# Neighbourhood attention on one core: the gate projections before the modulation products, instead of the two interleaved head by head

## The reference, cut to what matters

```python
mod = silu_c @ w_ada[layer] + b_ada[layer]                   # 6 * 1024 columns
sh_m, sc_m, gt_m, sh_f, sc_f, gt_f = jnp.split(mod, 6, axis=-1)
h = _rmsnorm(x, g_mix_pre[layer]) * (1.0 + sc_m[:, None]) + sh_m[:, None]
...
(na_k, na_v, ml_k, ml_v, ml_g, na_q, ml_q, ml_o, gate_na, gate_ml) = _split(h @ w_in[layer], IN_SPLITS)
...
o_na = _neighbourhood_attention(na_q, na_k, na_v, na_kc, na_vc, rpb[layer])
o_ml = _mlstm_branch(...)
merged = (jax.nn.sigmoid(gate_na) * (o_na @ w_branch_na[layer])
          + jax.nn.sigmoid(gate_ml) * (o_ml @ w_branch_ml[layer]))
x = x + gt_m[:, None] * _rmsnorm(merged @ w_out[layer], g_mix_post[layer])
```

## Time and profile before

| | us |
|---|---|
| median of 3 runs | 2588.36 |
| lowest, highest | 2583.66, 2589.1 |
| profiled execution, its own time | 2588.36 |
| its span, first to last instruction | 2586.4 |
| TensorE busy | 2296.2 (89%) |
| VectorE busy | 763.5 (30%) |
| ScalarE busy | 627.7 (24%) |
| the 16 iterations of attention, from the span's start | 255.0 to 385.0 |

### The profile page before, as it was taken

The page is one execution under the profiler, slowest core; times in us unless marked ns, Lnnn a source line. Parts: engine busy times, 40 slices in busy tenths (PEclk is TensorE's granted clock), DMA queues, the critical chain, the costliest instruction groups (busy, mean ns, idle before and its releaser), DMA issues.

```text
span 2586.4 us, 31263 instructions
## 1 busy us (share of the span) xinstructions
PE 2296.2 (89%) x13190; PEld 1587.1 (61%) x13190; DVE 763.5 (30%) x1251; ACT 627.7 (24%) x843; POOL 36.8 (1%) x23
## 2 busy tenths in 40 slices
PE   4999997769988988998899869999799699997997
PEld 2468666643333333333333349998799699986997
DVE  1001224241111111121111145443354445442453
ACT  2101432021101101110111134431343334412432
POOL 2100000010000000000000000000000000000000
PEclk7996999969999999999999979999899799998998
DMA  9434352319999999999999957773154345541542
GB/s 277 69 129 144 129 214 83 132 73 428 428 428 427 427 428 428 426 428 428 426 428 427 410 139 158 157 233 107 66 180 171 124 154 155 191 153 66 181 155 89
DMA packets 135924, 626.96 MB, mean 242 GB/s; under 512 B 11244, under 2 KB 19052, under 8 KB 110956
## 3 DMA queue, kind: packets, MB, share of 16 engines
q1 hardware_dynamic: 128384, 621.92, 63.6%
q0 software_dynamic: 1056, 0.20, 0.7%
q10 hardware_dynamic: 6348, 2.81, 0.5%
HBM read 623.69 MB, written 1.05 MB: 242 GB/s over the span
## 4 chain that ended last, share of the span: by engine, by line
PE 68%; DMA 20%; DVE 5%; ACT 3%; issue 2%; ACTq 1%; SPq 0%; DVEq 0%
DMA ring<-in_w_lin 18%; PE bank L1305 14%; PE bank L1051 12%; PE bank L1405 12%; PE bank L1587 10%; PE bank L1602 5%; PE bank L1066 2%; DMA ring<-in_w_ada 1%; ACTq L759 1%; PE bank L1117 1%; DMA ring<-in_w_in 1%; PE bank L1414 1%; PE bank L1293 1%; PE bank L1318 1%; PE bank L1138 1%
## 5 line engine op out<-in xcount | busy, mean ns | idle before, releaser
L1305 PE MATMUL bank<-ring,arenaA 128*64 128x512 f32 x3072 | 694.0, 602 | 37.8 <-DMA ring<-in_w_lin 26.1
L1305 PEld LDWEIGHTS bank<-ring,arenaA 128*64 128x64 f32 x3072 | 211.4, 138 | 461.5 <-issue 392.0
L1051 PE MATMUL bank<-arenaA,ring 128*128 128x256 f32 (+1 forms) x1408 | 339.8, 402 | 14.5 <-ACT arenaA L660 9.2
L1405 PE MATMUL bank<-arena_rounded,ring_rounded 128*128 128x256 f32 x2688 | 334.5, 285 | 9.3 <-ACT arena_rounded L837 7.9
L1405 PEld LDWEIGHTS bank<-arena_rounded,ring_rounded 128*128 128x128 f32 x2688 | 326.2, 191 | 14.2 <-issue 11.0
L1978 DVE TENSOR_TENSOR ring_rounded<-ring,ring_rounded 128x2048 fp32r<-128x2048 f32 (+1 forms) x140 | 293.4, 2133 | 134.1 <-ACT ring_rounded L829 134.0
L1051 PEld LDWEIGHTS bank<-arenaA,ring 128*128 128x128 f32 x1408 | 270.1, 193 | 86.3 <-issue 36.1
L829 ACT ACTIVATE ring_rounded<-ring 128x2048 fp32r<-128x2048 f32 (+1 forms) x140 | 243.0, 1784 | 317.2 <-DMA ring<-in_w_in 93.0
L1587 PE MATMUL bank<-arena_rounded,ring_rounded 128*128 128x256 f32 x2112 | 256.9, 285 | 8.0 <-ACT arena_rounded L954 8.0
L1587 PEld LDWEIGHTS bank<-arena_rounded,ring_rounded 128*128 128x128 f32 x2112 | 256.5, 193 | 8.6 <-issue 8.6
L1926 DVE TENSOR_SCALAR arenaA<-bank 128x512 f32<-128x512 f32 x32 | 22.1, 691 | 508.3 <-PE bank L1305 508.3
(11 more groups left out here) (338 smaller groups left out, 1640.7 us busy)
## 6 DMA issues: line engine op xcount, KB each, us to landing
ring<-in_w_gate SPq DMA_DIRECT2D x64, 2048.0 KB, 23.1
ring<-in_w_lin SPq DMA_DIRECT2D x64, 2048.0 KB, 25.5
ring<-in_w_down SPq DMA_DIRECT2D x64, 2048.0 KB, 21.5
ring<-in_w_in SPq DMA_DIRECT2D x41, 2048.0 KB, 10.8
ring<-in_w_ada SPq DMA_DIRECT2D x12, 2048.0 KB, 15.3
ring<-in_w_ffn_gate SPq DMA_DIRECT2D x10, 2048.0 KB, 7.9
ring<-in_w_ffn_up SPq DMA_DIRECT2D x10, 2048.0 KB, 7.8
ring<-in_w_ffn_down SPq DMA_DIRECT2D x12, 1536.0 KB, 6.4
```

The lines of the kernel that those rows point to most:

```text
L1051: last = pe.matmul(dst, w[:, c, base + m * P:base + (m + 1) * P], rhs(c), start=(c == 0), stop=(c == kc - 1))
L1305: last = pe.matmul(bank[b][k * SLOTS:(k + 1) * SLOTS, :], lhsT(c), slot(j)[:, c % 4, k * 512:(k + 1) * 512], start=False, stop=(c == DC - ...
L1405: last = pe.matmul(b[:, j * T:(j + 1) * T], w[:, c, m * P:(m + 1) * P], h[:, c, :], start=(part == 0 and c == 0 and j == 0), stop=(part == ...
```

## The change

It moves the filler work. Iterations 0 to 7 now each hold one whole gate group (16 matmuls), emptied by ScalarE in the same iteration. Iterations 8 to 15 each hold one whole modulation slab: `ada(i - 4)` and straight behind it `ada_turn(i - 4)`, with ScalarE's `ada_copy(i - 4)` behind the exponential of i, and VectorE's `modulation(i - 4)` ahead of the reciprocal and scaling of i. The slab list and the group list are put in the same order: four gate slabs and then eight modulation slabs. No arithmetic, no size and no operand changes.

```diff
@@ slabs
-        for k, (nm, c0) in enumerate((("gna0", C_GNA), ("gna1", C_GNA + 512), ("gml0", C_GML), ("gml1", C_GML + 512))):
-            slabs += [(nm, w_in[:, :, c0:c0 + 512])]
-            slabs += [(f"ada{i}", w_ada[:, :, 512 * i:512 * i + 512]) for i in (4 + 2 * k, 5 + 2 * k)]
+                  ("gna0", w_in[:, :, C_GNA:C_GNA + 512]), ("gna1", w_in[:, :, C_GNA + 512:C_GML]),
+                  ("gml0", w_in[:, :, C_GML:C_GML + 512]), ("gml1", w_in[:, :, C_GML + 512:C_GML + 1024])]
+        slabs += [(f"ada{i}", w_ada[:, :, 512 * i:512 * i + 512]) for i in range(4, 12)]
@@ groups
-        for k, name in enumerate(GATES):
-            groups += [("act", name), ("dve", f"ada{4 + k}")]
+        groups += [("act", f"gna{m}") for m in range(4)] + [("act", f"gml{m}") for m in range(4)]
+        groups += [("dve", f"ada{i}") for i in range(4, 12)]
@@ ScalarE, iteration i, behind the exponential of i
-                if qt == 0:
-                    ada_copy(4 + h)
-                else:
-                    if i == 1:
+                if i >= 8:
+                    ada_copy(i - 4)
+                if i < 8:
+                    name = filler[i]
+                    if i == 0:
                         act.wait_ge(sum_done, 1)
-                    dst = (gNA if h < 4 else gML)[:, 2 * (h % 4):2 * (h % 4) + 2, :]
-                    empty(GATES[h], dst, ACT.Sigmoid, src=two)
+                    dst = (gNA if i < 4 else gML)[:, 2 * (i % 4):2 * (i % 4) + 2, :]
+                    empty(name, dst, ACT.Sigmoid, src=two)
@@ TensorE
+            fillers = []
+            for nm, i in [(a, i) for a in ("gna", "gml") for i in range(4)]:
+                def f(nm=nm, i=i):
+                    w = slab(f"{nm}{i // 2}")
+                    pair(f"{nm}{i}", w, i % 2, lat)
+                fillers.append(f)
+            for i in range(4, 12):
+                fillers.append(lambda i=i: (ada(i), ada_turn(i)))
...
-                gate_half(i // 2, i % 2)
-                if i % 2 == 0:
-                    ada(4 + i // 2)
-                else:
-                    ada_turn(4 + i // 2)
+                fillers[i]()
@@ VectorE, iteration i
                 if i + 1 < 2 * NA_H:
                     front(i + 1)
+                if i >= 8:
+                    modulation(i - 4)
                 dve.wait_ge(na_exp, i + 1)
                 link(dve.reciprocal(nst[:, 32 + i:33 + i], nst[:, 32 + i:33 + i]))
                 dve.tensor_scalar(Pna[:, i % 2, :], Pna[:, i % 2, :], nst[:, 32 + i:33 + i], None, ALU.mult).then_inc(na_p, 1)
                 if qt:
-                    modulation(4 + h)
```

More of the change, by code:

```diff
@@ L496, in build @@
                   ("ml_q", w_in[:, :, C_MLQ:C_MLO]), ("ml_o", w_in[:, :, C_MLO:C_GNA]),
-                  ("rel0", A["rel"][:, 0:4096]), ("rel1", A["rel"][:, 4096:8192])]
-        for k, (nm, c0) in enumerate((("gna0", C_GNA), ("gna1", C_GNA + 512), ("gml0", C_GML), ("gml1", C_GML + 512))):
-            slabs += [(nm, w_in[:, :, c0:c0 + 512])]
-            slabs += [(f"ada{i}", w_ada[:, :, 512 * i:512 * i + 512]) for i in (4 + 2 * k, 5 + 2 * k)]
+                  ("rel0", A["rel"][:, 0:4096]), ("rel1", A["rel"][:, 4096:8192]),
+                  ("gna0", w_in[:, :, C_GNA:C_GNA + 512]), ("gna1", w_in[:, :, C_GNA + 512:C_GML]),
+                  ("gml0", w_in[:, :, C_GML:C_GML + 512]), ("gml1", w_in[:, :, C_GML + 512:C_GML + 1024])]
+        slabs += [(f"ada{i}", w_ada[:, :, 512 * i:512 * i + 512]) for i in range(4, 12)]
         slabs += [("b_na", A["w_branch_na"][0].rearrange("(c p) n -> p c n", p=P)),
@@ L520, in build @@
         groups += [("act", f"ml_o{m}") for m in range(2)]
-        GATES = [f"gna{m}" for m in range(4)] + [f"gml{m}" for m in range(4)]
-        for k, name in enumerate(GATES):
-            groups += [("act", name), ("dve", f"ada{4 + k}")]
+        groups += [("act", f"gna{m}") for m in range(4)] + [("act", f"gml{m}") for m in range(4)]
+        groups += [("dve", f"ada{i}") for i in range(4, 12)]
         groups += [("dve", f"b_na{m}") for m in range(4)] + [("dve", f"b_ml{m}") for m in range(4)]
@@ L689, in _ @@
             act.activation(lsg[:, :, :], gt2[:, :, :], ACT.Ln, bias=1.0).then_inc(g_exp, 1)
+            filler = [f"gna{m}" for m in range(4)] + [f"gml{m}" for m in range(4)]
             for i in range(2 * NA_H):
```

## The result

The changed kernel is slower: 2629.34 us median (2620.42 to 2630.68, 4 runs) against 2588.47 (2583.66 to 2589.1, 4 runs) for the kernel before, a ratio of 1.0155 with a 95% interval of 1.0129 to 1.0182. The direction was forecast, the size was not: 2611 was predicted, with 2622 as the upper end.

What follows compares the result with a forecast made beforehand. The loop was taken to be bound by TensorE's own work. Waits of 7.0 and 7.9 us, less 0.5 for the table load, make 14.4; with 8 us of clock on 2588.4 that gave 2611 us, range 2600 to 2622.

Steps and rivals of the forecast that it cites:

- Where the loop is bound, and that it is handed on: Attention loop: bound by TensorE's own work; a loop ending x us later delays the first expert slab's release by x.
- The DMA row: Profile page: transfers run at a share of 0.9 or more only from slice 9 on, behind the loop's slices 3 to 5.
- The waits: Iterations 8 to 15: ada to ada_turn 0.88 us, ada_turn to transposes 0.98 us, eight times each: 7.0 and 7.9 us.
- the table load: First head: the table load moves from iteration 1 to 0, where no values product follows: -0.5 us, ends 0 and -0.6.
- the dense heads: Iterations 0 to 7: one whole gate group each, heads of 20.4 us, nothing new waits, 0 us from the work's amount.
- the 0.1 us for the copy behind the sigmoid: Iterations 0 to 7: possible delay of the copy, 0.1 us for each of four odd iterations; taken as 0.
- The clock: Loop's second half: two to five falls to 1.2 GHz, middle 3.5, at 2.3 us each: 8 us, the least certain term.
- Rival B: Iterations 8 to 15: a clock fall in each, 13 to 24 us on top of 14.4: 2616 to 2627 us; chance 0.16.
- The stage behind the loop: mLSTM stage: no loss priced; its two falls cost 4.6 us, which a later start might save.
- rival D: mLSTM stage: later start moves its two falls elsewhere, gaining up to 4.6 us, 5.1 with table load: 2583 us; chance 0.02.
- The rule of the Trainium skill: Iterations 8 to 15: short matmul bursts between waits are throttled at each burst; alone, a fall in each iteration.
- transfers: Modulation slabs in the ring: ada10 can start six iterations before its use, against 15.3 us to landing: 0 us.

Runs made afterwards that it cites:

- dummies everywhere: Changed kernel with dummy matmuls in both new waits of the loop and in the mLSTM stage's waits: 2596.53 us, ratio 1.0024 to the kernel before.
- the kernel before with its own: Kernel before with dummy matmuls in the waits of the mLSTM heads and behind the last: 2584.11 us, ratio 0.9983 to the kernel before.
- after, mLSTM filled: Changed kernel with dummy matmuls in the mLSTM stage's waits only: 2619.29 us, ratio 1.0129 to the kernel before.
- the two kernels with only one wait: Changed kernel with modulation back behind the scaling, 2605.75 us; changed kernel with ada_turn one iteration later, 2604.02 us; both ratio 1.0054.
- the old order with the waits: Kernel before, but ada and ada_turn together in the odd iteration and modulation ahead of the scaling: 2622.39 us, ratio 1.0126.
- the one with the second wait filled: Changed kernel with one dummy matmul an iteration, behind ada_turn: 2607.08 us, ratio 1.0070 to the kernel before.
- The kernel with only modulation's wait: Changed kernel with ada_turn one iteration later, behind the next ada, modulation still ahead of the scaling: 2604.02 us, ratio 1.0054.
- the one with the first wait filled: Changed kernel with one dummy matmul an iteration, between ada and ada_turn: 2620.25 us, ratio 1.0115 to the kernel before.
- the kernel with only the copy's wait: Changed kernel with modulation behind the scaling again, ada and ada_turn still neighbours: 2605.75 us, ratio 1.0054 to the kernel before.

## Why the prediction was wrong, point by point

**Where the loop is bound, and that it is handed on**: right. The release of the first expert slab moved by 44.4 us of 44.9. The DMA row was read too simply: it has a 9 in slice 0 too, and the slices of the loop are averages (share 0.94 in the head from 323.23 to 338.99 of the kernel before). What decides is the chain, in which no transfer stands.

**The waits**: right in mechanism, and near in size. The prediction counted 14.4 us for both less the table load. With the clock taken out by dummies everywhere, the changed kernel stands 12.4 us over the kernel before with its own (2596.53 - 2584.11), 10.6 by the two ratios (0.41% of 2588), and 13.8 by the two profiled loops (143.4 - 129.6). That includes 0.06 us an iteration which the dummies add. Each pair of waits costs a little more than counted (1.98 for 1.86, 1.0 us in all), and the dense heads gain what I hadn't counted, 20.4 - 19.87 = 0.5 us each, 2 us, although the 0.1 us for the copy behind the sigmoid, which the prediction took at 0, is there. So part of the nearness is luck: two errors offset each other.

**The clock**: this is the step that failed, in the words of the prediction "I count on two to five falls, middle 3.5, at 2.3 each: 8 us". The mechanism was right and the term was mis-sized. The loop of the profiled execution has six low stretches, and they cost 164.5 - 143.4 = 21 us, 3.5 each; by the medians it is 2619.29 - 2596.53 = 23, by the ratios 27. I had guessed the number of falls from the mLSTM stage, where the gaps are shorter, and taken the price from its two disturbed heads. There a low stretch lasted under 7 us. In the new loop poor stretches recur every few us, some of them while the clock is still low: 49 us at the low level in six stretches of 3.6 to 13.6 us, some 8 us each. The number of stretches is a poor measure: the same loop in the execution of "after, mLSTM filled" has eight, but only 34 us at the low level, and costs 158.5 - 143.4 = 15 us. The time at the low level fits both, some 0.43 us of loss for each us of it. Rival B, a fall in each iteration for 13 to 24 us, described the loop better than the forecast did, though its 2616 to 2627 doesn't reach 2629 either. It had a chance of 0.16, and the prediction argued against it that the low level brings the clock back. It came back each time, and was lost again.

**The stage behind the loop**: missed. The prediction let the mLSTM stage keep its clock or gain (rival D) and gave no price to a loss. In the profile it is 8.7 us longer, at 0.80. By the medians the change costs there what its dummies save more in the changed kernel than in the kernel before: (2629.34 - 2619.29) - (2588.84 - 2584.11) = 5.3 us; by the ratios it is 2.3. The interval of the changed kernel's ratio alone is 7 us to either side, so this term isn't clear of nothing. How much of it stems from entering the stage at the low level, as the profiled execution did, and how much from where the executions happen to fall, one profile each doesn't settle: the two kernels with only one wait entered it at a high level and took 86.9 us too.

The three terms make 12.4 + 22.8 + 5.3 = 40.5 us. That they add up to about the 40.9 between the medians checks nothing: they are differences of the same five medians, and the sum is 2629.34 - 2588.84 by construction. By the ratios the terms are 10.6, 27 and 2.3.

**The rule of the Trainium skill** (TensorE: Matmul & The Clock Gate, section HAM oscillation — how this bites in real kernels), that bursts of matmuls between waits are throttled again and again, is borne out in part: by the changed kernel, six low stretches in eight iterations, and by the old order with the waits, seven in eight heads, but not by the kernels with one wait, two in eight iterations each, nor by the one with the second wait filled, none. As the prediction took it, it would have given 2616 to 2627 by the prices in the mLSTM stage, closer than the forecast. The section's case is of waits for transfers, longer than the waits of this loop; here TensorE was idle for only 0.72 and 0.85 us at a time, with a turn and transposes between.

**Table load, transfers**: right as far as seen. No wait for a modulation slab stands in the chain of the second half.

**Open.** What makes a stretch poor isn't settled. The kernel with only modulation's wait and the one with the first wait filled leave nearly the same stretch (turn 0.9 to 1.0, wait 0.83, transposes 0.66), yet have two and seven low stretches, 2604.02 and 2620.25 us. The latter's iteration is longer by one dummy. That turn and transposes are poor themselves was argued, not tested alone. With the same copy's wait and turn, the kernel with only the copy's wait, in which the transposes follow, has two low stretches, and the one with a dummy behind the turn none. How many falls a kernel has varies between executions, and each has one profile.

## What to carry to other kernels

Before two dependent steps of different engines are put next to each other, ask what stood between them. Here it was half a gate group and an iteration, and it hid a copy and a bias for nothing. Price such a wait twice: by its length, and by the clock, which cost here about twice the waits themselves in the loop, and perhaps more behind it. Count the time at the low level, not the falls. If a wait can't be hidden, idle TensorE time may be filled with matmuls that nobody reads, into a free bank: in the loop's waits it took back 27 us of 41, and in the mLSTM stage some 4 us of a kernel that had no fault otherwise.

## What the runs showed of the hardware that was not expected

Two waits of about 0.9 us, eight times each, cost 14 us each when alone and 40 together. A wait of 0.72 us followed by the turn's 1.05 and a dummy left the clock at its high level in all eight iterations of the profiled execution; with `modulation`'s wait of 0.85 and the transposes' 0.66 behind them in the dummy's place it was 0.69 on average. Dense work on both sides doesn't prevent it: in the old order with the waits, gate matmuls stand ahead of the poor stretch, and the granted clock behind it read 0.53 for 7 us.
